# S5 tables of a hybrid encoder: kernel products two steps at a time on four column strips, skip term added by PE

## What is computed

```python
bb_re = coef_re[..., None] * b_re - coef_im[..., None] * b_im      # and bb_im alike
bu_re = jnp.einsum('bsgc,gnc->bsgn', ug, bb_re)
# h: associative scan of  h = lam * h + bu  over the sequence
y = jnp.einsum('bsgn,gcn->bsgc', h_re, c_re) - jnp.einsum('bsgn,gcn->bsgc', h_im, c_im)
y = y.reshape(b, s, d) + d_skip.astype(F32) * hf
```

## Time and profile before

| what | value |
|---|---|
| median of 3 runs | 2591.61 us (2590.16 to 2595.8) |
| profiled execution, its own time | 2589.27 us |
| its span | 2587.4 us |
| mean granted PE clock over the span | 0.977 |
| busy PE, DVE, ACT, POOL | 2449.2, 1676.6, 1293.7, 221.7 us |
| the stage with the table steps | about 59 to 214 us of the span |

### The profile page before, as it was taken

One profiled execution on the slowest core, in us unless ns is written; L12 is line 12 of the kernel. 1 busy time (PEld: TensorE's weight loads), 2 busy tenths in 40 slices (PEclk: granted clock), 3 DMA queues, 4 the chain that ended last, 5 costly groups with the idle time before them and its releaser, 6 DMA issues.

```text
span 2587.4 us, 31654 instructions
## 1 busy us (share of the span) xinstructions
PE 2449.2 (95%) x12566; PEld 1975.3 (76%) x12566; DVE 1676.6 (65%) x2031; ACT 1293.7 (50%) x1508; POOL 221.7 (9%) x236
## 2 busy tenths in 40 slices
PE   7999998999999999689699999999999999999987
PEld 4445555588888876678599888998899988998856
DVE  7997676322223343872566788668876788667865
ACT  3644343222222233662355676557765577556753
POOL 4116633000000000000100000000000000000010
PEclk9999999999999999889799999999999999999998
DMA  7567310433323223441487799779987799777961
GB/s 201 172 192 228 102 65 25 162 98 98 98 98 106 98 90 126 164 183 37 168 273 249 269 371 332 252 248 324 367 304 244 244 361 368 265 248 260 375 248 45
DMA packets 316818, 527.72 MB, mean 204 GB/s; under 512 B 19334, under 2 KB 175594, under 8 KB 314010
## 3 DMA queue, kind: packets, MB, share of 16 engines
q1 hardware_dynamic: 287594, 481.30, 53.9%
q0 software_dynamic: 5888, 25.78, 3.2%
q10 hardware_dynamic: 23184, 18.55, 2.2%
HBM read 496.03 MB, written 45.81 MB: 209 GB/s over the span
## 4 chain that ended last, share of the span: by engine, by line
PE 82%; DVE 9%; ACT 3%; issue 2%; POOL 2%; DMA 2%; ACTq 0%; POOLq 0%; DVEq 0%
PE psum L1922 28%; PE psum L1448 17%; PE psum L1982 12%; PE psum L1747 5%; PE psum L1984 5%; PE psum L1336 3%; PE psum L1310 2%; PE psum L2082 2%; PE psum L1520 1%; DVE stages L870 1%; DVE stages L880 1%; DVE stages L875 1%; DVE stages L871 1%; POOL stages L1126 1%; POOL stages L1129 1%
## 5 line engine op out<-in xcount | busy, mean ns | idle before, releaser
L3524 DVE TENSOR_TENSOR stages_r<-kept,stages_r 128x2048 fp32r<-128x2048 f32 x336 | 769.3, 2291 | 238.6 <-ACT stages_r L2536 237.8
L2536 ACT ACTIVATE stages_r<-kept 128x2048 fp32r<-128x2048 f32 x336 | 637.4, 1912 | 217.8 <-PE psum L1922 104.2
L1922 PE MATMUL psum<-stages_r 128*128 128x512 f32 x3136 | 738.8, 394 | 3.2 <-issue 3.2
L1922 PEld LDWEIGHTS psum<-stages_r 128*128 128x128 f32 x3136 | 584.2, 189 | 126.5 <-issue 4.8
L1982 PE MATMUL psum<-stages_r 128*128 128x320 f32 x1792 | 465.1, 346 | 4.1 <-DVE stages L3557 3.1
L1448 PE MATMUL psum<-stages_r 128*128 128x512 f32 x1920 | 437.5, 390 | 3.3 <-ACT stages_r L2109 2.7
L1984 PE MATMUL psum<-stages_r 128*128 128x160 f32 x1792 | 423.8, 236 | 0.0
L1448 PEld LDWEIGHTS psum<-stages_r 128*128 128x128 f32 x1920 | 360.2, 188 | 79.2 <-ACT stages_r L2109 3.1
L1984 PEld LDWEIGHTS psum<-stages_r 128*128 128x128 f32 x1792 | 344.0, 192 | 2.0
L3176 DVE TENSOR_TENSOR stages_r<-kept,stages_r 128x2048 fp32r<-128x2048 f32 x54 | 123.8, 2293 | 338.7 <-ACT stages_r L2394 338.7
L1982 PEld LDWEIGHTS psum<-stages_r 128*128 128x128 f32 x1792 | 337.6, 188 | 6.8 <-DVE stages_r L3524 3.8
(11 more groups left out here) (452 smaller groups left out, 2467.7 us busy)
## 6 DMA issues: line engine op xcount, KB each, us to landing
kept<-in_moe_w_gu_dram SPq DMA_DIRECT2D x224, 1024.0 KB, 6.7
kept<-in_moe_w_down_dram SPq DMA_DIRECT2D x112, 1024.0 KB, 6.6
kept<-in_ffn_w_gu_dram SPq DMA_DIRECT2D x28, 1024.0 KB, 5.2
kept<-in_ev_w_in_dram SPq DMA_DIRECT2D x16, 1024.0 KB, 8.1
kept<-in_ffn_w_down_dram SPq DMA_DIRECT2D x14, 1024.0 KB, 5.0
s_output_maps<-s_output_maps_by_state SPq DMA_DIRECT2D x32, 256.0 KB, 4.6
kept<-s_input_maps SPq DMA_DIRECT2D x8, 1024.0 KB, 5.7
kept<-s_output_maps SPq DMA_DIRECT2D x8, 1024.0 KB, 6.2
```

The source lines that it names most:

```text
L1922: m = pe.matmul(out_, a, b, start=start and n == 0, stop=stop and n == len(pairs) - 1, skip_group_check=True)
L2536: act.activation(w_high[n % WSLOTS], unit_tile(n), ACT.Copy).then_inc(s_wh, 1)
L3524: dve.tensor_tensor(w_low[n % WSLOTS], unit_tile(n), w_high[n % WSLOTS], ALU.subtract).then_inc(s_ws, 1)
```

## The change

- PE takes two steps at a time. Before the products of an even k from 2 on: `b_step(k-2)`, `b_step(k-1)`, `kernel_steps(k-2, 2)`; at k = 31 `b_step(30)`, `b_step(31)` and `kernel_steps(30, 1)`; two products before the end `kernel_steps(31, 1)`. In `kernel_steps` the products of both steps for one direction follow each other, so that four strips are used in turn.
- The skip term is a matmul of its own on PE: Dm (16 rows) times the 16x16 identity, accumulated on the columns of difference 0, one for each group. POOL's `add_skip` and its semaphore are gone; the store follows the copy.
- DVE's six operations of a step are in another order: both products of the input map, both of the output map, then the two sums. The waits for a result just issued are gone, and the two log operations of a block stand behind the products of the next step.
- ACT copies two steps at even k, and stores the input map one step later; the counts of stores are changed to match.

```diff
@@ kernel_bank, STORED
-        STORED = [16 * (3 * (0 < k) + (k >= 2) + (k == NSTEP)) for k in range(NSTEP + 1)]
+        STORED = [16 * (2 * (0 < k) + 2 * (k >= 2) + 2 * (k == NSTEP)) for k in range(NSTEP + 1)]
@@ POOL
-            chain.link(pool.tensor_tensor(Dm[0:GC, :, :], Dm[0:GC, :, :],
-                                          ident[0:GC, 0:GC].unsqueeze(1).broadcast_to([GC, G5, GC]), ALU.mult))
+            pool.tensor_tensor(Dm[0:GC, :, :], Dm[0:GC, :, :],
+                               ident[0:GC, 0:GC].unsqueeze(1).broadcast_to([GC, G5, GC]), ALU.mult).then_inc(s_dw, 1)
...
-            def add_skip(k):
-                pool.wait_ge(s_kc, k + 1)
-                m = KJ[k % 3][0:GC, :, L5 - 1, :]
-                pool.tensor_tensor(m, m, Dm[0:GC, STEP * k:STEP * (k + 1), :], ALU.add).then_inc(s_kd, 1)
@@ PE, dense_block and s5_step
-                            kernel_step(NSTEP - 1)
+                            kernel_steps(NSTEP - 1, 1)
...
-                b_step(k)
-                if k:
-                    kernel_step(k - 1)
+                if k == NSTEP - 1:
+                    b_step(k - 1)
+                    b_step(k)
+                    kernel_steps(k - 1, 1)
+                elif k and k % 2 == 0:
+                    b_step(k - 2)
+                    b_step(k - 1)
+                    kernel_steps(k - 2, 2)
...
+            def kernel_steps(k0, n):
+
+                steps = range(k0, k0 + n)
+                pe.wait_ge(s_bc, 2 * (k0 + n))
+                if k0 >= 2:
+                    pe.wait_ge(s_kc, k0 + n - 2)
                 for d in range(2):
+                    for k in steps:
+                        for g in range(STEP):
+                            pe.matmul(kernel_bank(k, g, GC * (L5 - 1) * (1 - d), P),
+                                      BP[k % 3][:, g, d, (L5 - 1) * (1 - d), :],
+                                      CP[k % 3][:, g, d, d:d + L5, :].rearrange("p m c -> p (m c)"), start=d == 0, stop=False,
+                                      skip_group_check=True)
+                if k0 == 0:
+                    pe.wait_ge(s_dw, 17)
+                for k in steps:
                     for g in range(STEP):
+                        m = pe.matmul(kernel_bank(k, g, GC * (L5 - 1), GC), Dm[0:GC, STEP * k + g, :], ident[0:GC, 0:GC],
+                                      start=False, stop=True, skip_group_check=True)
+                    m.then_inc(s_kk, 1)
@@ ACT
-                act.wait_ge(s_kd, k + 1)
+                act.wait_ge(s_kc, k + 1)
...
-                    b_copy(k)
-                    if k:
-                        b_store(k - 1)
+                    if k >= 2:
+                        if k % 2 == 0:
+                            b_copy(k - 2)
+                            b_copy(k - 1)
+                            kernel_copy(k - 2)
+                            kernel_copy(k - 1)
+                        b_store(k - 2)
+                        kernel_store(k - 2)
+                    if k == NSTEP - 1:
+                        b_copy(k - 1)
                         kernel_copy(k - 1)
@@ DVE, powers(k, behind=None), in the order of its operations
...
+                if k:
+                    dve.wait_ge(s_bc, 2 * k - 1)
...
-                chain.settle()
-                dve.tensor_tensor(BP[k % 3], BP[k % 3], BQ, ALU.add).then_inc(s_bc, 1)
+                inputs_done = chain.n
+                if behind is not None:
+                    behind[0]()
...
+                if k:
+                    dve.wait_ge(s_bc, 2 * k)
...
-                chain.settle()
+                outputs_done = chain.n
+                if behind is not None:
+                    behind[1]()
+                dve.wait_ge(chain.sem, inputs_done)
+                dve.tensor_tensor(BP[k % 3], BP[k % 3], BQ, ALU.add).then_inc(s_bc, 1)
+                dve.wait_ge(chain.sem, outputs_done)
                 dve.tensor_tensor(CP[k % 3], CP[k % 3], CQ, ALU.add).then_inc(s_bc, 1)
```

More of the change, by code:

```diff
@@ L308, in build_program @@
         s_c3 = sem("s5_c_block_loaded")
-        s_dw = sem("s5_skip_loaded")
+        s_dw = sem("s5_skip_loaded_then_ready")
         s_sin = sem("s5_sin_ready")
@@ L323, in build_program @@
         s_kc = sem("s5_kernels_copied")
-        s_kd = sem("s5_kernels_with_skip")
         s_mv = sem("s5_tables_laid_out")
@@ L1409, in b_step @@
                 m.then_inc(s_bt, 1)
[L1411 to L1415, removed]
-                for d in range(2):
-                    for g in range(STEP):
[L1418 to L1422, removed]
+            def kernel_steps(k0, n):
[3 more added lines that the diff above has]
+                    pe.wait_ge(s_kc, k0 + n - 2)
+                for d in range(2):
+                    for k in steps:
[7 more added lines that the diff above has]
+                for k in steps:
+                    for g in range(STEP):
+                        m = pe.matmul(kernel_bank(k, g, GC * (L5 - 1), GC), Dm[0:GC, STEP * k + g, :], ident[0:GC, 0:GC],
+                                      start=False, stop=True, skip_group_check=True)
+                    m.then_inc(s_kk, 1)
             def split_product(run, behind={}):
@@ L2201, in b_store @@
                 act.wait_ge(s_big, k + 1)
-                act.dma_start(s5_big[k // 4][:, 512 * (k % 4):512 * (k % 4 + 1)], Bstage[k % 3]).then_inc(s_tst[(k + 1) % 2], 16)
+                act.dma_start(s5_big[k // 4][:, 512 * (k % 4):512 * (k % 4 + 1)], Bstage[k % 3]).then_inc(s_tst[min(k + 2, NSTEP) % 2], 16)
             def kernel_copy(k):
@@ L2247, in _ @@
                     tables_stored(act, NSTEP - 2)
+                    b_copy(NSTEP - 1)
+                    b_store(NSTEP - 2)
                     b_store(NSTEP - 1)
@@ L2303, in _ @@
                     tables_stored(act, NSTEP)
-                    act.wait_ge(s_kd, NSTEP)
+                    act.wait_ge(s_kc, NSTEP)
                     act.wait_ge(s_bc, 2 * NSTEP)
@@ L2847, in _, with logs_of, logs_split, logs_floor @@
                 m.then_inc(s_rc, 1)
-            def logs_in(d, b):
-                dve.wait_ge(s_k, 4 * d + b + 1)
-                if d:
-                    dve.wait_ge(s_lf, 1)
-                chain.link(dve.tensor_scalar(lnb4[:, b, :], lf[d][:, b, :], 1.0 / LN_SPLIT, 1.0, ALU.mult, ALU.min))
-                chain.settle()
-                dve.tensor_scalar(lf[d][:, b, :], lf[d][:, b, :], LN_SPLIT, None, ALU.max).then_inc(s_lnin, 1)
+            def logs_of(d, b):
+                split_done = []
+                def logs_split():
+                    dve.wait_ge(s_k, 4 * d + b + 1)
+                    if d:
+                        dve.wait_ge(s_lf, 1)
+                    chain.link(dve.tensor_scalar(lnb4[:, b, :], lf[d][:, b, :], 1.0 / LN_SPLIT, 1.0, ALU.mult, ALU.min))
+                    split_done.append(chain.n)
+                def logs_floor():
+                    dve.wait_ge(chain.sem, split_done[0])
+                    dve.tensor_scalar(lf[d][:, b, :], lf[d][:, b, :], LN_SPLIT, None, ALU.max).then_inc(s_lnin, 1)
+                return logs_split, logs_floor
             def logs_out(d):
@@ L2860, in logs_out, with powers @@
                 dve.tensor_tensor(lf[d], lf[d], lnb4, ALU.add).then_inc(s_lf, 1)
-            def powers(k):
+            def powers(k, behind=None):
                 g0, gb = STEP * k, STEP * k % 8
@@ L2895, in _ @@
             dve.wait_ge(s_s5in, 64)
+            logs_behind = None
             for k in range(NSTEP):
-                powers(k)
+                powers(k, logs_behind)
+                logs_behind = None
                 for d in range(2):
                     if LOGS_IN[d] <= k < LOGS_IN[d] + 4:
-                        logs_in(d, k - LOGS_IN[d])
+                        logs_behind = logs_of(d, k - LOGS_IN[d])
                     if k == LOGS_OUT[d]:
@@ L2912, in diag_scores @@
                     tables_stored(dve, NSTEP)
-                    dve.wait_ge(s_kd, NSTEP)
+                    dve.wait_ge(s_kc, NSTEP)
                 dve.tensor_tensor(S_diag[hd % 2], psum[:, v % 3, :].rearrange("p (c t) -> p c t", c=TC),
```

8 lines of the change are left out of this document (removed).

## The result

The changed kernel takes 2576.38 us (median of five runs, 2575.14 to 2580.65) where the kernel before takes 2591.61 (2590.16 to 2595.8 in five). The ratio is 0.9946, with a 95% interval of 0.9935 to 0.9957: about 14 us faster by the ratio (the two medians lie 15.2 apart), where 9.3 was forecast. The profiled execution took 2575.14 us with a span of 2573.5, 13.9 less than before.

A forecast was written before the change was run, and what follows sets the result against it. PE and DVE were both taken as full, with PE staying the bound. 5.1 us of PE work plus 4.2 us of waits made 9.3 us, from the 2591.6 us median to 2582.3 us, range 2577.5 to 2588.5.

The forecast's parts named there:

- The sum: Whole stage with the table steps: 5.1 us less PE work plus 4.2 us fewer waits, 9.3 us gained.
- The pair block: PE's strips and skip term per pair: 0.74 + 0.37 = 1.11 us instead of 1.48, saving 0.37, 15 times.
- Waits: PE's 8.4 us of standing: 4.2 go; 1.5 stay at the first pair, 2.7 in three slow-store stretches.
- PE stays the bound: Table-step stage: PE's work falls to 138.9 us, 4.15 per step against DVE's 3.84, so PE still bounds.
- One of the signs set down as fatal: Profile after: a chain running over DVE between 70 and 200 us would prove the prediction wrong at the root.
- DVE's order: DVE's six operations per step: 4.06 us falls to 3.84; with the logs DVE gives back 7.8 us in all.
- 0.6 us longer for the first transposes: First step: BP's sum stands behind C products that wait for ACT, so PE's transposes come 0.6 us later.
- POOL bounds nothing: POOL, busy about 2 us in 20, binds nothing; removing its 0.23 us last addition does not shorten the path.
- Only two strips: Rival, PE's strip block: only two strips go at once, 6.6 us more work; gain 4.7, 2586.9 us; chance 0.17.
- DVE and the stores take the gain: Rival, pair hand-over: slow store landings make DVE and PE wait; gain about 4, 2587.5 us; chance 0.10.
- Strips one by one: Rival, PE's strip block: each strip instruction takes its own round; kernel 7 us slower, 2599 us; chance 0.06.
- The gain does not reach the end: Rival, behind the stage: something due at a fixed time swallows the gain, 2591 us; chance 0.05.

The follow-up runs named there:

- e4: The kernel before with only the skip term moved from POOL to PE, step by step, DVE in the old order: 2593.29 us.
- e2: The changed kernel with DVE's old order put back; PE in pairs and skip term on PE stay: 2583.38 us.
- e7: The changed kernel with the first direction's strip products done three times instead of once, 7.5 us more PE work: 2582.62 us.
- e1: The kernel before with only DVE's new order; PE, ACT and POOL as before: 2604.23 us.
- e11: The changed kernel with the skip term back on POOL as an addition: 2602.81 us.
- e9: e1 with one wait put back per step, so that CP's sum waits for the end of BP's: 2597.27 us.
- e6: The changed kernel with ACT copying the first block of C before the four operations of bounded_forget instead of behind them: 2579.01 us.
- e5: The changed kernel with the strip products back in the old program order, the first step's before the second's: 2576.7 us.
- e10: The kernel before with DVE's new order and the skip term left out, PE step by step: 2597.53 us.
- e12: e10 with ACT's copies of the first block of C issued before bounded_forget: 2593.33 us.
- e3: e2 with POOL's addition of the skip term kept, so PE in pairs alone against the kernel before: 2584.77 us.

## Why the prediction was right, and where it wasn't

**The sum.** 9.3 us were forecast at the stage's end; 14.3 came, and 13.9 in the span. The range went down to 2577.5: the median of 2576.38 lies 1.1 below it, the time by the ratio (2577.6) at its very edge. So the direction and most of the mechanism were right and the size was too small by a third. By the forecast's own count (from the end of the last product before the first step to the end of the last product) the stage takes 138.2 us, of which 2.5 are PE's waits and 135.7 work, against 8.4 and 144.0. So work fell by 8.3 instead of 5.1, and waits by 5.9 instead of 4.2. (By the count of the table the waits before are 8.0, so 5.5 and 8.7.)

**The pair block: right mechanism, one term too dear.** Four strips side by side, 0.56 us for 16 instructions: as forecast. The skip term was put at 0.37 us by the row at line 1510 with bounds of 0.15 and 0.80; it costs 0.16, practically the change of shape alone. The nearest row in form was twice too dear; e4 gives 0.14 for four of the small instructions, the block above 0.16 for eight, so their number hardly counts. Why the four at line 1510 take longer no run tells. A pair saves 1.48 - 0.56 - 0.16 - 0.19 = 0.57 us instead of 0.37. With 15 pairs this is 3.0 of the 3.2 us.

**Waits.** The places were right: none before 69 us, little behind. The three stretches with slow stores (2.7 us) did not come. Stores still take up to 6.0 us to land, but none of them was the last thing that DVE waited for.

**PE stays the bound: wrong, without harm.** The sum took DVE at 3.84 us a step as having slack beside PE's 4.15 (which leaves out PE's transposes for C and the decays; with them its 138.9 us are 4.34 a step). But DVE also has the logs and `logs_out`: from its first C product at 63.59 to the end of its last sum at 194.17 it runs 130.6 us without a stop, or 4.08 a step, and all of PE's work measured 4.24. Stretches of 20.00 and 20.00, e2 and e7 all say that both bound. One of the signs set down as fatal, a chain over DVE between 70 and 200 us, did come: its largest DVE lines alone hold over 40% of the chain there. It was a bad sign. Where two engines are both full, the chain takes now one, now the other, and says nothing against the gain.

**DVE's order.** Its size was right, 0.22 us a step; from e2 to the changed kernel DVE's last sum moves up by 7.8 us (201.32 to 193.50), as forecast for DVE's work, and the stage gets 6.5 of them. What failed was costing it by itself. "0.6 us longer for the first transposes" was 3.0 in e1 (4.59 us of wait instead of 1.62), since the C products behind which the sum was put wait for ACT. In the changed kernel most of that is hidden: PE has products until 69 us.

**POOL bounds nothing: wrong in its reason.** By rows 1 POOL was busy for 2 us in 20, and by rows 9 one addition takes 0.23. Both were true of a DVE with gaps. The forecast took POOL's engine time for its whole cost; in e11 single additions stay open for up to 7.11 us beside the new order. The forecast closed DVE's gaps and, without having seen it, removed the one operation that suffers from it. That the change gained in spite of this is luck. Had the skip term stayed on POOL, the same order would have ended at 2603, slower than before (e11). No rival named this, though it decides the sign of the change's middle part.

**The rivals.** Only two strips: false (0.56 us for 16). DVE and the stores take the gain: false, though e2 looks like it; its "about 4" doesn't follow either, since 1 us in half of 15 pairs would leave 1.8 of the 9.3. Strips one by one: false. The gain does not reach the end: false, 13.9 of 14.3 do.

## What to carry to other kernels

When two engines are full in the same stretches, cost a change on both and on every combination of its parts: here pairs alone gain 7.4 us, DVE's order alone loses 10.6, together with the moved addition they gain 14.3. Before closing DVE's gaps, look for small POOL instructions that run beside DVE and for who waits behind them; moving them to an engine with room comes first. And a sum moved behind other operations inherits their waits, above all in the first step, where nothing has been prefetched.

## What the runs showed of the hardware

- A POOL addition of 16x32 elements with inputs in SBUF can stay open as long as DVE works through its queue without a gap: up to 9.27 us in e1 and 7.11 in e11, where 0.23 to 0.87 is usual. It happened to 14 of the 40 that lay in such work or ended at its end; the other 26 ended about 0.1 us behind a DVE instruction. With a DVE gap of 0.1 us in each step (e9) none of 32 was long. The other way round, a DVE product beside a POOL operation that started first took 1.91 us instead of 0.76 (e6).
- Matmuls of 16 columns on four column strips start in rounds of four, 0.11 us apart, whatever their order in the program (e5). Eight matmul instructions of 16 rows, 16 columns and 16 moving columns on those strips lengthen the block by 0.16 us all together, the change of shape included.
- After PE had stood for 4.4 us the granted clock fell to 0.50 for 3.4 us (e1, e10), and after 2.8 us also (e12, 0.57 as the mean of 64 to 68 us). In the kernels before and after, with waits of 1.46 and 0.85 us at these places, it stayed at 1.00. The length of the stop alone doesn't decide: after 1.58 us up to 115.79 it fell in e3 (0.60 as the mean of 116 to 120 us), after 2.35 us up to 169.71 it stayed at 1.00 in e1.
